# Branch A's 64x64 products of a two-layer decoder kernel: issued in pairs on all four quarters of the PE array

## What is computed

```python
    def step(S, inp):
        r_t, w_t, k_t, v_t, kk_t, b_t = inp
        sk = jnp.einsum('bhvk,bhk->bhv', S, kk_t)
        S = S * w_t[:, :, None, :] - sk[..., None] * b_t[:, :, None, :] + v_t[..., None] * k_t[:, :, None, :]
        return S, jnp.einsum('bhvk,bhk->bhv', S, r_t)
...
def _layer(x, pos, s_wkv, s_ret, s_shift, p):
    h = _rmsnorm(x, p['norm_mix_pre'])
    z = h @ p['w_in']
...
    m = jax.nn.sigmoid(ga) * (ya @ p['w_out_a']) + jax.nn.sigmoid(gb) * (yb @ p['w_out_b'])
    x = x + _rmsnorm(m @ p['w_o'], p['norm_mix_post'])
```

## Time and profile before

| | |
|---|---|
| device time, median of 3 runs | 1342.22 us (1341.97 to 1342.58) |
| the profiled execution's own time | 1344.05 us |
| span in its trace, first to last instruction | 1342.3 us (1.75 us lie around it) |
| mean granted clock of PE | 0.984 |

### The profile page before, as it was taken

One profiled execution on the slowest core, in us unless ns is written; L12 is line 12 of the kernel. 1 busy time (PEld: TensorE's weight loads), 2 busy tenths in 40 slices (PEclk: granted clock), 3 DMA queues, 4 the chain that ended last, 5 costly groups with the idle time before them and its releaser, 6 DMA issues.

```text
span 1342.3 us, 27273 instructions
## 1 busy us (share of the span) xinstructions
PE 1288.2 (96%) x11888; PEld 1218.3 (91%) x11888; DVE 900.5 (67%) x1550; ACT 517.6 (39%) x737; POOL 14.7 (1%) x26
## 2 busy tenths in 40 slices
PE   6999999999998999999989999999999989999996
PEld 5899997889997999999878999978999979999996
DVE  3887768687776556653468876669776766656533
ACT  4553032445435433333445520233444354333432
POOL 0001000000000000000000020000000000000000
PEclk9999999999998999999989999999999989999998
DMA  5433123544443544544423322245443534444442
GB/s 203 142 108 132 41 92 120 182 151 156 142 144 123 169 154 145 156 145 155 142 74 119 125 97 68 81 143 192 141 144 130 167 114 136 149 151 148 154 145 71
DMA packets 51175, 179.49 MB, mean 134 GB/s; under 512 B 6256, under 2 KB 7024, under 8 KB 49776
## 3 DMA queue, kind: packets, MB, share of 16 engines
q1 hardware_dynamic: 41904, 150.49, 35.3%
q10 hardware_dynamic: 9152, 27.25, 5.9%
HBM read 166.57 MB, written 8.53 MB: 130 GB/s over the span
## 4 chain that ended last, share of the span: by engine, by line
PE 89%; DVE 5%; ACT 3%; DMA 1%; issue 1%; ACTq 0%; SPq 0%; DVEq 0%
PE dense L1138 51%; PE core L1138 38%; DVE w_lo L693 1%; ACT w_hi L438 1%; DVE x L741 1%; DVE y_out L739 1%; ACT L426 0%; DMA ret_s<-ret_t 0%; DMA x<-x_t 0%; DVE bonus L804 0%; DVE tmp L790 0%; DVE bonus L800 0%; PE core L1299 0%; DVE h_lo L697 0%; DVE zs L801 0%
## 5 line engine op out<-in xcount | busy, mean ns | idle before, releaser
L693 DVE TENSOR_TENSOR w_lo<-w_raw,w_hi 128x1024 fp32r<-128x1024 f32 x282 | 344.8, 1223 | 255.7 <-ACT w_hi L438 254.5
L438 ACT ACTIVATE w_hi<-w_raw 128x1024 fp32r<-128x1024 f32 x282 | 297.7, 1057 | 564.7 <-PE dense L1138 428.0
L1138 PE MATMUL dense<-h_hi,w_hi 128*128 128x320 f32 x1296 | 418.4, 323 | 26.1 <-DVE h_lo L697 14.6
L1138 PE MATMUL dense<-h_hi,w_lo 128*128 128x320 f32 x1296 | 405.7, 313 | 0.0
L1138 PE MATMUL dense<-h_lo,w_hi 128*128 128x320 f32 x1296 | 405.6, 313 | 0.0
L1138 PEld LDWEIGHTS dense<-h_hi,w_hi 128*128 128x128 f32 x1296 | 248.0, 191 | 43.4 <-issue 31.4
L1138 PEld LDWEIGHTS dense<-h_lo,w_hi 128*128 128x128 f32 x1296 | 248.4, 192 | 2.1
L1138 PEld LDWEIGHTS dense<-h_hi,w_lo 128*128 128x128 f32 x1296 | 248.1, 191 | 0.0
L1138 PE MATMUL core<-h_hi,w_hi 128*128 128x320 f32 x416 | 129.7, 312 | 4.2 <-DVE w_lo L693 4.2
L1138 PE MATMUL core<-h_hi,w_lo 128*128 128x320 f32 x416 | 129.0, 310 | 0.0
L1138 PE MATMUL core<-h_lo,w_hi 128*128 128x320 f32 x416 | 129.0, 310 | 0.0
(11 more groups left out here) (250 smaller groups left out, 1843.8 us busy)
## 6 DMA issues: line engine op xcount, KB each, us to landing
w_raw<-wts SPq DMA_DIRECT2D x282, 512.0 KB, 3.5
ret_t<-ret_t ACTq DMA_DIRECT2D x16, 256.0 KB, 4.0
ret_s<-ret_t ACTq DMA_DIRECT2D x16, 256.0 KB, 2.4
ret_rest<-ret_d ACTq DMA_DIRECT2D x2, 1536.0 KB, 7.8
qk_rot<-qk_raw ACTq DMA_DIRECT2D x8, 320.0 KB, 6.0
dmask<-rconst ACTq DMA_DIRECT2D x2, 1152.0 KB, 5.7
s_st<-wkv_st ACTq DMA_DIRECT2D x2, 1024.0 KB, 5.4
wkv_s<-s_st ACTq DMA_DIRECT2D x2, 1024.0 KB, 3.9
```

Of the source, the lines that this page charges most:

```text
L438: act.activation(w_hi[n % RING][:, :], w_raw[n % RING][:, :], ACT.Copy).then_inc(hi_ready.sem, 1)
L693: dve.tensor_tensor(w_lo[r][:, :], w_raw[r][:, :], w_hi[r][:, :].bitcast(F32), ALU.subtract).then_inc(low_made.sem, 1)
L1138: return pe.matmul(out, lhsT, rhs, start=start, stop=stop)
```

## The change

`across` is a product whose rows 0-63 write output rows 64-127 and the other way round. The rounds become 94 jobs in a written table of 48 slots (`ROUNDS`, of which the diff shows the first line). A slot names one job that runs as `halves` and one that runs `across`, and PE alternates them block by block. Three streams (`FLIP` = 1, 2, 3) have `e` and `dt` turned, `vt`, `kt` and the k part of the old `tok` (`tk`) run across. A job uses bank number (place in the list) mod 8, the dense banks too. ACT now empties `vt`, `tk`, `tb`, all `e` above level 0 without a mask, and `m` of the three streams (whose masked `x` comes from a second product, `mx`); POOL makes the masks into `p_sq` copies of `m_sq`. In the sequence the products with v (`w'`, `y'`, `s'`) run across beside another step's products, are emptied by ACT into SBUF and added by DVE. Sample states go to two banks, one across; POOL decays the old ones. Dense tiles from `T_V` to `T_GATE`+3 rotate over two banks; one `v_tile` moves from behind `w` of chunk 2 to the end of the rounds. The sums of the opening move to one step (4 in layer 0, 6 in layer 1), the third `high` behind the root, and the first `q_exp` ahead of two `low`.

```diff
+SUMS_AT = (4, 6)
...
+FLIP = (1, 2, 3)
+ROUNDS = ("vt0", "mt0 mx1", "mt1 mx2", "mt2 mx3", "mt3 kt0", "m0 kt1", "m1 kt2", "m2 kt3", "m3 e01", "mt4 e02", "e00 e03",
...
+    return name in ("vt", "tk", "tb") or (name == "e" and lv > 0) or (name == "m" and s in FLIP)
...
-VALUES_AFTER = [("w", 0), ("u", 0), ("ys", 0), ("w", 1), ("u", 1), ("w", 2), ("u", 2), ("w", 3)]
+VALUES_AFTER = [("w", 0), ("u", 0), ("ys", 0), ("w", 1), ("u", 1), ("u", 2), ("w", 3)]
...
+BESIDE = {("u", 0): [("y'", 0), ("s'", 0)], ("as0", SAMPLE): [("w'", SAMPLE)], ("as1", SAMPLE): [("y'", SAMPLE)]}
+for _c in range(1, NCHUNK):
+    BESIDE |= {("ys", _c - 1): [("w'", _c)], ("w", _c): [("s'", _c)], ("u", _c): [("y'", _c)]}
...
+            if T_V <= g < T_GATE + 4:
+                return dense[(g - T_V) % 2]
...
+        def state_banks(h):
+
+            return (core[3], core[2]) if h % 2 else (dense[2], core[4])
...
+        def round_bank(job):
+
+            return banks[(JOB_AT[job] - 1) % 8]
...
+                        if lv >= 3:
+                            pool.wait_ge(*round_done(layer, JOB_AT["e", lv - 2, s]))
+                        pool.tensor_tensor(pairs(p_sq[lv % 2], s, C), pairs(m_sq, s, C), mask(M_LOW + C * (lv - 1)), ALU.mult)\
+                            .then_inc(round_p.sem, 1)
+                    else:
...
+                pool.wait_ge(*seq_done(layer, SEQ_AT["as3", SAMPLE]))
+                for h in range(HP):
+                    s3 = s0_st[:, h * 512:(h + 1) * 512].rearrange("p (s c) -> p s c", s=NSEQ)
+                    pool.tensor_tensor(s3, s3, bc(seq_decay[:, h * NSEQ:(h + 1) * NSEQ], 2, C), ALU.mult).then_inc(old_decayed.sem, 1)
...
                     act.wait_ge(*x_partial(layer, k))
                     act.activation(acc[:, :], core[0][:, 0:T], ACT.Copy).then_inc(x_parted.sem, 1)
-                    if k == 1:
-                        high(RING)
                     act.wait_ge(*x_summed(layer, k))
                     inverse_root(root[:, :], core[0][:, 0:T], 1.0 / D, eps(0)).then_inc(x_rooted.sem, 1)
 
 
                 x_root(1)
+                high(RING)
...
+                for job in A_OPS:
+                    name, lv, s = job
+                    act.wait_ge(*round_done(layer, JOB_AT[job]))
+                    to = {"vt": pairs(v_st, s, C), "m": pairs(m_sq, s, C), "e": pairs(e_sq, s, C),
+                          "tk": pairs(tok, s, 128)[:, :, 0:C], "tb": pairs(tok, s, 128)[:, :, C:2 * C]}[name]
+                    act.activation(to, round_bank(job)[:, 0:256].rearrange("p (m c) -> p m c", m=4), ACT.Copy).then_inc(round_a.sem, 1)
...
-                for n in (1, 2):
-                    low(layer, T_V + n)
...
+                dve.wait_ge(*round_v(layer, len(V_OPS)))
+                low(layer, T_V + 1)
...
                         decay = bc(chunk_decay[:, :].rearrange("p (h m) -> p h m", h=HP)[:, :, c], 2, C)
+                        dve.wait_ge(*aside_evac(layer, ASIDE_AT["y'", c]))
+                        dve.wait_ge(*aside_evac(layer, ASIDE_AT["s'", c]))
                         if c:
+                            link(dve.tensor_tensor(h4(s_st), h4(s_st), h4(s_v), ALU.add))
                             link(dve.tensor_tensor(h4(s_st), h4(s_st), pv64("s", c), ALU.add))
...
-                        dve.tensor_copy(c4(y_a)[:, :, c * C:(c + 1) * C], pv64("y", c)).then_inc(seq_evac.sem, 1)
+                            link(dve.tensor_tensor(h4(s_st), pv64("s", c), h4(s_v), ALU.add))
+                        dve.tensor_tensor(h4(s_st), h4(s_st), decay, ALU.mult).then_inc(seq_evac.sem, 1)
+                        y = c4(y_a)[:, :, c * C:(c + 1) * C]
+                        dve.tensor_tensor(y, y, pv64("y", c), ALU.add).then_inc(seq_evac.sem, 1)
...
-                        dve.tensor_tensor(s3, s3, bc(seq_decay[:, h * NSEQ:(h + 1) * NSEQ], 2, C), ALU.mult).then_inc(seq_evac.sem, 1)
+                        dve.wait_ge(*old_decayed(layer, h + 1))
+                        link(dve.tensor_tensor(st, st, state_banks(h)[0][:, :], ALU.add))
+                        dve.tensor_tensor(st, st, state_banks(h)[1][:, :], ALU.add).then_inc(seq_evac.sem, 1)
                     make_after(step)
 
...
+                        dve.wait_ge(*rcs_loaded(layer, 1))
+                        make_qexp(0)
...
-                make_qexp(0)
...
+                    pe.wait_ge(*x_squared(layer, (k - 1) * KT + 4 * half + 4))
                     for j in range(4):
                         c = 4 * half + j
-                        pe.wait_ge(*x_squared(layer, (k - 1) * KT + c + 1))
...
+                def sums():
+                    x_sum(1, 0)
+                    x_sum(1, 1)
+                at = SUMS_AT[layer > 0]
+                opening(0, 0, h_ready, 0, {at: sums, at + 1: lambda: x_pick(1)})
...
+                def across(out, lhsT, rhs, start=True, stop=True):
+
+                    mm(out[C:2 * C], lhsT[0:C], rhs[0:C], start, stop)
+                    return mm(out[0:C], lhsT[C:2 * C], rhs[C:2 * C], start, stop)
...
+                    name, lv, s = job
+                    if name == "e":
+                        need(masked_by_pool(layer, "p", lv, s) if lv else made(layer, ("m", 0, s)))
+                        need(made(layer, ("dt", lv - 1, s)) if lv else masked_by_pool(layer, "xt", 0, s))
+                    elif name in ("dt", "d"):
+                        need(made(layer, ("e", lv, s)))
...
+                    turned = across if s in FLIP else halves
...
+                        return across(ps64, stream(zs[:, 11 * T:15 * T], s)[:, m, :], i2)
                     if name == "mt":
...
+                        return halves(ps, b_st[:, b64], ar[:, b128])
+                    if name == "kt":
...
+                        return halves(ps64, b_dec[:, of] if s == HP else b_st[:, b64], i2)
+                    if name in ("m", "mx"):
+                        return (across if name == "mx" else halves)(ps64, ar[:, b128][:, 0:C], b_st[:, b64])
+                    if name == "e":
+                        return turned(ps64, (p_sq[lv % 2] if lv else m_sq)[:, b64], xt[:, b64])
+                    if name == "dt":
+                        return turned(ps64, x_sq[:, b64], e_sq[:, b64])
+                    return halves(ps64, e_sq[:, b64], x_sq[:, b64])
+
+                pe.wait_ge(*bonus_out(layer, HP))
+                for slot in ROUNDS:
+                    pair = [named(t) for t in slot.split()]
+                    for job in pair:
+                        n = JOB_AT[job] - 1
+                        if n >= 8:
+                            need(emptied(layer, JOBS[n - 8]))
+                        elif n == len(core):
+                            pe.wait_ge(*evacuated_by(layer, T_V - 1))
+                        operands(job)
                     for m in range(4):
...
-                        ps = core[s][:, m * 128:(m + 1) * 128]
-                        ps64 = core[s][:, m * C:(m + 1) * C]
-                        if name == "vt":
...
-                pe.wait_ge(*round_evac(layer, N_ROUNDS))
+                for b in (len(core), len(core) + 1):
+                    need(emptied(layer, max((j for j in JOBS if round_bank(j) is banks[b]), key=JOB_AT.get)))
+                v_tile()
+                need(round_v(layer, len(V_OPS)))
+                need(round_a(layer, len(A_OPS)))
...
+                    def beside(h):
...
+                        for what, cc in BESIDE.get((name, c), []):
...
+                            if what == "w'":
+                                ins = across(ps, step_mats(makt, cc, C)[:, h, :], step_mats(v_st, cc, C)[:, h, :])
...
+                            else:
+                                ins = across(ps, step_mats(tok, cc, 128)[:, h, 0:C], step_mats(v_st, cc, C)[:, h, :])
...
+                    if (name, c) in BESIDE:
+                        first = ASIDE_AT[BESIDE[name, c][0]]
+                        if first > 1:
+                            pe.wait_ge(*aside_evac(layer, first - 1))
...
-                    if h == 1:
+                    if h == 0:
                         pe.wait_ge(*v_tok_ready(layer, 8))
-                    if h >= 2:
+                        evac("ys", NCHUNK - 1)
+                    elif h == 1:
+                        evac("y", SAMPLE)
+                    else:
                         evac(f"s{h - 2}", SAMPLE)
                     tk = step_mats(tok, SAMPLE, 128)[:, h, :]
-                    halves(core[3 + h % 2][:, :], tk[:, 0:C], v_exp[h % 2][:, :], True, False)
-                    done(halves(core[3 + h % 2][:, :], tk[:, C:2 * C], u_exp[h % 2][:, :], False, True))
+                    of_u, of_v = state_banks(h)
+                    across(of_v[:, :], tk[:, 0:C], v_exp[h % 2][:, :])
+                    done(halves(of_u[:, :], tk[:, C:2 * C], u_exp[h % 2][:, :]))
```

More of the change, by code:

```diff
@@ L177, in program @@
         opened = dense + core[3:5]
+        banks = core + dense
         def bank(g):
@@ L353, in kind, with made, emptied, masked_by_pool @@
```

(74 more changed lines are left out.)

266 lines of the change are left out of this document (149 added, 117 removed), and 4 rows, old and new, of the table ROUNDS.

## The result

The changed kernel takes 1331.19 us (median of 4 runs, 1327.99 to 1334.42) against 1342.24 us before: ratio 0.9915, interval 0.9903 to 0.9928, 11 us less. The forecast was 1294 us with a range from 1281 to 1311: it is faster, as forecast, but by less than a quarter of the 48 us, and outside the range.

A forecast was written before the change was run, and what follows sets the result against it. PE was taken to bound the kernel, busy for 96% of the span. Rounds 36.4, opening 4.2 and behind the rounds 7.6 sum to 48.2 us; from the median of 1342.22 that gave 1294 us, range 1281 to 1311.

The forecast's parts named there:

- 26.4 + 1.8 + 0.5 = 28.7 us: Rounds, each layer: PE's slots 26.4, waits for DVE in early slots 1.8, waits one slot behind 0.5; stage 28.7 us.
- The overlap that it assumed: Rounds: a crossed pair costs PE one block's time, 0.119 us, or 0.219 with `mt` or `kt`, instead of 0.238 without overlap.
- 18.2 twice: Rounds: 28.7 us instead of 46.9 saves 18.2 us in each layer, 36.4 in all.
- issue is the bound: Rival: each record has a price of some 27 ns, so four quarters gain nothing in narrow slots; 1334 us, chance 0.10.
- Emptying becomes the bound: Rival: same overlap, but DVE or POOL takes its upper price, giving rounds of 33 us; 1303 us, chance 0.15.
- no overlap: Rival: a crossed product waits for its partner because they share rows, so the change is slower; 1352 us, chance 0.07.
- The opening: Before tile 3: PE's 2.11 us wait for DVE's `w_lo` goes; gain 2.1 us in each layer, 4.2 in all.
- Behind the rounds: From the rounds' end on: gains 11.8 less new waits 8.0, net 3.8 us a layer, 7.6 in all.
- 5.7 + 3.6: Behind the rounds, PE time saved each layer: v products leaving PE's queue 5.7 us, sample states' two products running at once 3.6.
- The products set aside: Behind the rounds: v products must be emptied by ACT before the next step's; five waits of 0.7, 3.5 us a layer.
- The third variance: Branch A's norm, two banks instead of three: it waits for ACT's logarithm of the first, about 2.5 us.
- the clock at 1.2 GHz in the rounds: Sign of being wrong: PE's granted clock at 1.2 GHz in the rounds, for which the holes before give no reason.

The follow-up runs named there:

- e3: Changed kernel with one product of twice the columns for two neighbouring blocks in the rounds, halving PE instructions (result not the reference's): 1299.79 us.
- e10: Changed kernel with eight DVE operations of branch A's gated output moved from the middle of the retention's first pair to its end: 1330.4 us.
- e5: Changed kernel with four dense value tiles of the sequence put into the rounds as eight pieces of 12 products, DVE's rotations and weight splits moved: 1325.55 us.
- e11: e5 with e10's move on DVE, the pieces three slots later and DVE's weight splits out of slots 2 to 12: 1318.28 us.
- e1: Changed kernel with the two jobs of a slot issued one after the other instead of block by block: 1330.95 us.
- e4: Changed kernel with four dense value tiles of the sequence spread over the rounds as 32 pieces of three products, in a bank of their own: 1339.32 us.
- e6: Changed kernel with the first gate tile ahead of sample state 0, that state's wait for the last `ys` removed, two retention transfers earlier: 1335.0 us.

## Why the prediction was wrong

**The rounds, the step that failed.** "26.4 + 1.8 + 0.5 = 28.7 us" prices each slot by the columns in the array and by the engines that empty banks. It put the delivery of PE's instructions at nothing, without a reason: only a price of each record stands in it, as a rival. The overlap that it assumed is real (0.47 a slot), as are DVE's waits (e3: 1.4 us of them, stage 29.3 and 28.8). But the change keeps 3008 instructions a layer and halves the time in which they are used. 3008 instructions are 11.75 packets; at the 3.66 us that one takes on average they account for 43 of the 44.7 us. The gain is 2.2 and 1.65 us, not 18.2 twice. The 32.5 us between are the whole of the miss between the two traces (48.2 forecast, 16.1 measured), and e3 gives 31.6 of them back (15.4 and 16.2). By the medians the miss is 5 us larger; that part is scatter of the executions.

The material was there: 1456 products and as many loads in 46.90 us are 256 instructions in 4.1 us, and the instruction queue's packets lie in the view of DMA queues. The Trainium skill, "Runtime: NRT & Kernel Launch", section "Instruction fetch mechanics", says that instructions come in blocks of 256, fetched while the block before is executed, and that this stays hidden because dispatch is slower than the refill. The blocks agree with this trace (256 instructions from standstill to standstill, 16 KB a packet); hidden the fetch is in the kernel before, where a block lasts 3.68 us, and not at 1.9.

**The rival "issue is the bound"** came out near in its number (1334) and wrong in its mechanism. Records within a packet start 0.0146 us apart on average, so 27 ns are no price of a record; the time is lost in one halt for every 128 products. The 25 ns of the Trainium skill, "TensorE: Matmul & The Clock Gate", section "Wait — 56ns, not 53.3ns?", are undercut by these rows too. "Emptying becomes the bound" and "no overlap" fall with e3 and with the 0.47.

**The opening** gave 3.65 and 2.8 us, not 2.1. The wait for `w_lo` is gone as forecast. Besides, the two groups of strips now follow each other, so PE no longer changes twice between strips and full products, and in layer 0 full products come to their faster pace sooner (starts 0.27 us apart up to 19.6 us before, 0.15 from 18.5 us now). PE in order of time, before and then after:

```profile
17.87 0.64 PE L1138 MATMUL dense<-h_hi,w_hi 128*128 128x320 f32 x1
18.30 0.47 PE L1138 MATMUL dense<-h_lo,w_hi 128*128 128x320 f32 x1
```

```profile
18.25 0.41 PE L1255 MATMUL dense<-h_hi,w_hi 128*128 128x320 f32 x1
18.50 0.31 PE L1255 MATMUL dense<-h_lo,w_hi 128*128 128x320 f32 x1
```

**Behind the rounds** 2.7 and 2.9 us were gained, where 3.8 were forecast: right in sign and nearly in size, but in part by luck. By the earlier trace rows and the same stretches now, PE is busy there for 6.3 us less in layer 0, not 9.3 (5.7 + 3.6), and stands still for 3.7 more, not 5.5: two errors that nearly cancel. What PE waited for there:

```profile
PE core L1255 <- DVE y_a L1021: 2.2, 1, 2.2
PE dense L1255 <- DVE y_a L1021: 1.0, 1, 1.0
PE core L1462 <- ACT v_tok L650: 0.7, 1, 0.7
PE core L1255 <- ACT sq_a L705: 0.6, 1, 0.6
...
PE core L1255 <- ACT s_v L665: 0.5, 1, 0.5
```

`s0` waits 2.2 us (2.0 forecast). The products set aside cost ACT waits of 0.3 to 0.5 in four places (3.5 in all forecast, 1.6 measured). The third variance waits 0.6, not 2.5. Waits that were not forecast make up for part of it (1.0 and 0.7). `q_exp` is in time, but the hole that stood there stands at `s0` now, and behind it PE's granted clock is 0.50 for 3.4 us, as it was behind the old hole. Before, then now:

```profile
248.40:251.80 3.40, 3.40 (x15) 3.40 (x14) 3.13 (x9) 0.00 (x0) 0.00 (x0) 0.50 0.97 403
...
212.03:215.44 3.41, 3.41 (x11) 2.16 (x8) 3.38 (x5) 0.00 (x0) 0.00 (x0) 0.50 0.98 318
```

The prediction had read the clock within the old hole (1.00) and not behind it; so it missed that these 3.4 us, which cost some 1.7 (an estimate, half of them), would move from the retention into the tail. In the rounds of this execution the clock stays at 1.00 through all eleven standstills, but in e10's it does not: what the prediction named as a sign of being wrong, the clock at 1.2 GHz in the rounds, can occur with the same rounds, and the stage is some 2 us longer where it does. In the retention the 1.7 us for `ret_t` were not forecast: PE comes earlier and DVE's list does not (e10). They take back what the clock no longer costs there: up to the first of `ya` it takes 103.1 and 102.8 us before, 103.1 and 103.1 now.

What stays open: why a packet's transfer starts only 1.05 to 1.86 us after PE has gone on, and why PE goes on only 2.17 to 2.65 us after that start, though the transfer itself lasts 0.9 to 1.2; and whether this chain can be shortened.

## What to carry to other kernels

Count instructions as a resource of its own. Where PE uses up 256 of them (products and weight loads together) in less than a packet's chain (3.4 to 4.3 us here), small products in more quarters of the array buy nothing; wider products, or full products between them in pieces large enough to pay for the change (0.36 us here), do (e3, e5, e11). And when a busy table shows every engine with room, look at the waits that end with "issue", at the rhythm of their ends, and at the instruction queue.

## What the runs showed of the hardware that was not expected

- In the rounds 256 instructions of PE come every 3.35 to 4.26 us (changed kernel, layer 0; 3.37 to 4.10 in e1), whatever PE does with them; it is hidden at 3.68 us of work (kernel before) and in the open at 1.9 (changed kernel) or 2.6 (e1).
- PE starts products of the next job on free quarters up to 0.17 us before the present job's have all started (e1). Alternating them by hand brought nothing measurable here, where delivery sets the pace.
- A change between 64x64 fp32 products and full ones and back costs about 0.36 us (e4).
- The changed kernel's four runs lie 6.4 us apart, those of the kernel before 0.6. The scatter goes roughly with the mean granted clock: 0.983 for the fastest of the four, 0.979 for the slowest; in e6 1328.07 us at 0.985 and 1336.94 at 0.975. e10's trace shows where it can fall, in the rounds with their standstills; why it does in one execution and not in another no run says.
